# Expert down weights loaded in 32 KB packets, two experts on even and odd partitions

## The reference, cut to what matters

```python
def run_block(args):
    xb, e = args
    h = jax.nn.silu(xb @ w_gate[e]) * (xb @ w_up[e])
    return h @ w_down[e]
```

## Time and profile before

| | us |
|---|---|
| median of 3 runs | 1330.17 |
| lowest and highest | 1329.52, 1331.28 |
| the profiled execution's own time | 1329.42 |
| its span, first to last instruction | 1327.6 |
| busy: TensorE products, VectorE, ScalarE | 966.9, 451.8, 281.9 |

### The profile page before, as it was taken

The page is one execution under the profiler, slowest core; times in us unless marked ns, Lnnn a source line. Parts: engine busy times, 40 slices in busy tenths (PEclk is TensorE's granted clock), DMA queues, the critical chain, the costliest instruction groups (busy, mean ns, idle before and its releaser), DMA issues.

```text
span 1327.6 us, 30597 instructions
## 1 busy us (share of the span) xinstructions
PE 966.9 (73%) x13784; PEld 668.0 (50%) x13784; DVE 451.8 (34%) x1013; ACT 281.9 (21%) x632; POOL 41.8 (3%) x38
## 2 busy tenths in 40 slices
PE   9999999999999876466475746647574664757474
PEld 6998778888866433233243423324342432434242
DVE  4798776788844221111010211101021111102121
ACT  5655343738332100000000010000000000000001
POOL 0000201011120000000000000000000000000000
PEclk9999999999999988788787878878797978879798
DMA  9562455235494999999999999999999999999996
GB/s 329 164 246 82 150 190 190 99 112 203 175 429 177 400 433 431 427 430 433 428 431 438 429 429 435 428 429 431 436 430 434 431 429 428 431 433 432 429 426 270
DMA packets 56023, 464.45 MB, mean 350 GB/s; under 512 B 6250, under 2 KB 15268, under 8 KB 37924
## 3 DMA queue, kind: packets, MB, share of 16 engines
q1 hardware_dynamic: 55040, 460.81, 83.5%
q10 hardware_dynamic: 932, 2.92, 0.6%
HBM read 462.67 MB, written 1.05 MB: 349 GB/s over the span
## 4 chain that ended last, share of the span: by engine, by line
DMA 47%; PE 43%; DVE 6%; ACT 1%; issue 1%; SPq 1%; POOL 0%; POOLq 0%; DVEq 0%; ACTq 0%
DMA second_set<-in_w_up 41%; PE bank L2234 15%; PE bank L2877 9%; DMA ring<-in_w_up 5%; PE bank L2786 5%; PE bank L2769 3%; PE bank L2188 3%; PE bank L2212 2%; DVE ring_lo L1380 1%; PE bank L2282 1%; PE bank L2391 1%; PE bank L2299 1%; PE bank L2416 1%; DVE expert_area L2040 1%; DVE qk L1351 1%
## 5 line engine op out<-in xcount | busy, mean ns | idle before, releaser
L2890 PE MATMUL bank<-consts 128*32 128x32 f32 x52 | 8.0, 247 | 237.9 <-DMA second_set<-in_w_up 170.7
L2234 PE MATMUL bank<-ring_lo,xt_hi 128*128 128x512 f32 (+3 forms) x544 | 171.9, 383 | 0.2 <-DVE ring_lo L1380 0.2
L2786 PE MATMUL bank<-ring,consts 128*32 128x256 f32 x1952 | 118.7, 382 | 69.7 <-DVE consts L2043 41.0
L1266 ACT ACTIVATE expert_area<-bank 128x128 f32<-128x128 f32 x64 | 15.0, 275 | 656.4 <-PE bank L2877 577.6
L2040 DVE TENSOR_TENSOR expert_area<-expert_area,bank 128x128 f32<-128x128 f32 x64 | 22.9, 358 | 340.0 <-ACT expert_area L1266 340.0
L2890 PEld LDWEIGHTS bank<-consts 128*32 128x32 f32 x52 | 4.7, 138 | 245.9 <-DMA second_set<-in_w_up 176.9
L2786 PEld LDWEIGHTS bank<-ring,consts 128*32 128x32 f32 x1952 | 62.7, 109 | 121.8 <-issue 59.9
L2877 PE MATMUL bank<-second_set,expert_area 64*32 64x256 f32 x3328 | 119.4, 452 | 1.1 <-issue 1.1
L2877 PE MATMUL bank<-ring,expert_area 64*32 64x256 f32 x3328 | 118.8, 452 | 0.0
L2234 PEld LDWEIGHTS bank<-ring_lo,xt_hi 128*128 128x128 f32 x544 | 99.1, 188 | 18.4 <-issue 1.5
L2877 PEld LDWEIGHTS bank<-second_set,expert_area 64*32 64x32 f32 x3328 | 70.5, 127 | 44.6 <-issue 26.9
(11 more groups left out here) (351 smaller groups left out, 1400.5 us busy)
## 6 DMA issues: line engine op xcount, KB each, us to landing
ring<-in_w_down SPq DMA_DIRECT2D x60, 2048.0 KB, 22.1
ring<-in_w_gate SPq DMA_DIRECT2D x13, 4096.0 KB, 31.6
ring<-in_w_up SPq DMA_DIRECT2D x13, 4096.0 KB, 40.7
second_set<-in_w_gate SPq DMA_DIRECT2D x13, 4096.0 KB, 32.4
second_set<-in_w_up SPq DMA_DIRECT2D x13, 4096.0 KB, 41.7
ring<-in_w_gate SPq DMA_DIRECT2D x7, 2048.0 KB, 17.7
ring<-in_w_up SPq DMA_DIRECT2D x6, 2048.0 KB, 22.1
ring<-in_moba_w_kv SPq DMA_DIRECT2D x4, 2048.0 KB, 8.4
```

The lines of the kernel that those rows point to most:

```text
L2234: last = nc.tensor.matmul(dst, x[at], w[:, c, :], start=(piece == 0 and c == 0 and w is hi and x is x_hi), stop=(piece == 1 and c == per - ...
L2786: last = nc.tensor.matmul(down_in[SLOTS * j:SLOTS * j + SLOTS, :], turned[:, SLOTS * k:SLOTS * k + SLOTS], w[k][:, 256 * j:256 * j + 256], ...
```

## The change

In the paired rounds the downs of a pair share one buffer, `ring` 4 and 5 together, 32 KB on each partition. The even expert takes the 64 even partitions and the odd expert the 64 odd ones; each is one DMA of 64 rows of 32 KB. A row of the new layout holds 8 of the 512 hidden features. The hidden rows of an expert are written into a 128 x 256 tile at every second column, the other columns being zero, so that after the turn in 32 x 32 blocks the expert's features stand on its own partitions and zeros on the other's. The down product of one expert then runs over all 128 rows of the shared buffer in 8 steps rather than 4. Both downs wait for both down products of the pair before, and TensorE waits for both loads ahead of the first product. Round 15's loads are reordered: gate and up of its first two experts, then their downs. The zero tiles lie in `early_down` and are cleared once on VectorE ahead of the paired rounds.

```diff
-        hidden_pair = [hidden, expert_area[:, 1152:1280]]
+        hidden_zeros = early_down[:, 2048:2560].rearrange("p (w n) -> p w n", w=2)
+        hidden_pair_t = early_down[:, 2560:3072].rearrange("p (w n) -> p w n", w=2)
+        down_pair = ring[:, 4:6, :].rearrange("p k n -> p (k n)")
...
+                frees[2]()
                 for parity in range(2):
-                    frees[2 + parity]()
-                    down(e + parity, ring[:, 4 + parity, :], down_landed[parity])
+                    src = t["w_down_2"][0, bass.ds(e + parity, 1)].rearrange("e (f k) n -> f (e k n)", k=2 * 4)
+                    sp.dma_start(down_pair[parity::2, :], src).then_inc(down_landed[parity], 16)
...
-                        load_pair(e, q, (used, used, down_taken(GROUP * r + (first + 2 * q - 1)),
-                                         down_taken(GROUP * r + (first + 2 * q))))
+                        load_pair(e, q, (used, used, down_taken(e)))
...
-            load_expert(e, 0, hidden_taken(e - 2), down_taken(e - 1))
-            load_expert(e + 1, 1, hidden_taken(e - 2), down_taken(e))
+            hidden_taken(e - 2)()
+            for i in range(2):
+                if i:
+                    hidden_taken(e)()
+                for k, name in enumerate(("w_gate_2", "w_up_2")):
+                    gate_or_up(name, e + i, ring[:, 2 * i + k, :], gate_up_landed[i])
+            down_taken(e)()
+            for i in range(2):
+                down(e + i, ring[:, 4 + i, :], down_landed[i])
...
+                own = hidden_zeros[:, of, :].rearrange("p (k q e) -> p k q e", k=8, e=2)[:, :, :, of]
+                nc.vector.tensor_tensor(own, *gate_up, ALU.mult).then_inc(hidden_ready, 1)
                 dve.wait_ge(hidden_ready, x + 1)
-                nc.vector.transpose(hidden_t_pair[of], hidden_pair[of]).then_inc(hidden_t_ready, 1)
+                nc.vector.transpose(hidden_pair_t[:, of, :], hidden_zeros[:, of, :]).then_inc(hidden_t_ready, 1)
...
+            nc.vector.memset(hidden_zeros, 0.0)
...
+            def down_of_pair(parity):
+
+                for k in range(8):
+                    for j in range(4):
+                        last = nc.tensor.matmul(down_in[SLOTS * j:SLOTS * j + SLOTS, :],
+                                                hidden_pair_t[:, parity, SLOTS * k:SLOTS * k + SLOTS],
+                                                down_pair[:, D * k + 256 * j:D * k + 256 * j + 256],
+                                                start=(k == 0), stop=(k == 7))
+                last.then_inc(down_in_psum, 1)
...
-                        pe.wait_ge(down_landed[parity], 32 * (n - 2) + (16 * q + 16))
+                        if parity == 0:
+                            for landed in down_landed:
+                                pe.wait_ge(landed, 32 * (n - 2) + (16 * q + 16))
                         if i:
                             down_drained(GROUP * n + i)
-                        down(ring[:, 4 + parity, :], range(4), hidden_t_pair[parity])
+                        down_of_pair(parity)
```

More of the change, by code:

```diff
@@ L336, in build @@
         hidden_t = unused[:, 1024:1152]
-        hidden_t_pair = [hidden_t, unused[:, 1408:1536]]
         onehot = unused[:, 1152:1408].rearrange("p (t s) -> p t s", t=2)
@@ L796, in fifth_used @@
                 down_taken(6)()
-            load_pair(8, 0, (hidden_taken(5), fifth_used, hidden_taken(6), down_taken(8)))
-            load_pair(10, 1, (hidden_taken(8), hidden_taken(7), down_taken(9), down_taken(10)))
+            load_pair(8, 0, (hidden_taken(5), fifth_used, down_taken(8)))
+            load_pair(10, 1, (hidden_taken(8), hidden_taken(7), down_taken(10)))
             load_further_pairs(3 * GROUP, ROUNDS - 4)
             e = NE - GROUP
-            load_expert(e, 0, hidden_taken(e - 2), down_taken(e - 1))
-            load_expert(e + 1, 1, hidden_taken(e - 2), down_taken(e))
+            hidden_taken(e - 2)()
[7 more added lines that the diff above has]
+                down(e + i, ring[:, 4 + i, :], down_landed[i])
             load_expert(e + 2, 0, hidden_taken(e + 1), down_taken(e + 1))
@@ L2034, in take_back, with hidden_of_pair, hidden_of @@
                 nc.vector.tensor_copy(back, back_in).then_inc(back_ready, 1)
-            def hidden_of(x, of=0):
+            def hidden_of_pair(x, of):
                 dve.wait_ge(silu_done, x + 1)
-                gate_up = [a.rearrange("p (q k) -> p k q", k=4)
+                gate_up = [a.rearrange("p (q k) -> p k q", k=8)
                            for a in (act_g_pair[of], hidden_pair_in[of][:, P:2 * P])]
-                nc.vector.tensor_tensor(hidden_pair[of].rearrange("p (k q) -> p k q", k=4), *gate_up,
-                                        ALU.mult).then_inc(hidden_ready, 1)
+                own = hidden_zeros[:, of, :].rearrange("p (k q e) -> p k q e", k=8, e=2)[:, :, :, of]
+                nc.vector.tensor_tensor(own, *gate_up, ALU.mult).then_inc(hidden_ready, 1)
                 dve.wait_ge(hidden_ready, x + 1)
-                nc.vector.transpose(hidden_t_pair[of], hidden_pair[of]).then_inc(hidden_t_ready, 1)
+                nc.vector.transpose(hidden_pair_t[:, of, :], hidden_zeros[:, of, :]).then_inc(hidden_t_ready, 1)
+            def hidden_of(x):
+                dve.wait_ge(silu_done, x + 1)
+                gate_up = [a.rearrange("p (q k) -> p k q", k=4) for a in (act_g, hidden_in[:, P:2 * P])]
+                nc.vector.tensor_tensor(hidden.rearrange("p (k q) -> p k q", k=4), *gate_up, ALU.mult).then_inc(
+                    hidden_ready, 1)
+                dve.wait_ge(hidden_ready, x + 1)
+                nc.vector.transpose(hidden_t, hidden).then_inc(hidden_t_ready, 1)
             def drain_down(n, i):
@@ L2078, in paired_round @@
                     for parity in range(2):
-                        hidden_of(GROUP * r + (2 * q + parity), parity)
+                        hidden_of_pair(GROUP * r + (2 * q + parity), parity)
                     for parity in range(2):
@@ L2779, in hidden_turned, with down @@
                 pe.wait_ge(hidden_t_ready, x + 1)
-            def down(down_w, chunks, turned=hidden_t):
+            def down(down_w, chunks):
                 w = down_w if isinstance(down_w, list) else [down_w[:, D * k:D * k + D] for k in range(4)]
@@ L2786, in down @@
                         last = nc.tensor.matmul(down_in[SLOTS * j:SLOTS * j + SLOTS, :],
-                                                turned[:, SLOTS * k:SLOTS * k + SLOTS],
+                                                hidden_t[:, SLOTS * k:SLOTS * k + SLOTS],
                                                 w[k][:, 256 * j:256 * j + 256], start=(k == 0), stop=(k == 3))
```

## The result

The changed kernel takes 1420.66 us (median of 4 runs, 1416.38 to 1421.97) against 1330.15 us of the kernel before measured beside it: a ratio of 1.0672, interval 1.0659 to 1.0685. That is 90.5 us slower, where 1.6 us faster was forecast, and far outside the range. The profiled execution took 1421.64 us, with a span of 1419.8 us.

The account below looks back on a forecast made before the run. The prediction took the paired rounds to be bound by the DMA engines. Larger packets save 1.56 us, all other terms cost nothing, so the median of 1330.17 us becomes 1328.6 us, range 1326.9 to 1334.0 us.

Parts of the forecast that it names:

- What bounds the kernel: Paired rounds of 58.17 us are bound by the DMA engines, DMA share 1.00; other engines wait once per pair.
- the packets: Paired downs: one 32 KB packet replaces two of 16 KB, saving 7.5 ns each, 1.56 us in all (1.1 to 2.4).
- The collision rival: Half-filled 64-row down transfers collide in memory, packets last twice as long: +253 us, 1583 us; chance 0.08.
- More products: Down products grow from 32 to 64 records; a pair is later by 3.5 to 4.5 us, costing nothing on the path.
- the cover: TensorE's idle time before gate and up, 13.1 us at `second_set` and 5.0 us at `ring`, hides the added products.
- Both loads before the first product: TensorE's wait for both downs of a pair adds at most 1 us, out of the same 8 us.
- Later issues: SP issues both downs behind both earlier products, still 8 us early; costs only if TensorE is late by over 8 us.
- The code rival: The paired rounds' longer code is fetched again, 7 packets in 12 rounds: +3.2 to +5.5 us, net +1.6 to +4; chance 0.25.
- No gain: Engine time goes by bytes alone, the 7.5 ns per packet being a recording artefact: 1330.2 us; chance 0.12.
- the small terms: Reordered first and last paired loads and the clearing on VectorE: put at nothing, reaching from 0 to +1 us.

Follow-up runs that it names:

- steps4: The changed kernel with 4 of 8 steps in each paired down product, half the hidden features left out: 1328.05 us, ratio 0.9985 to the kernel before.
- pair_product: The changed kernel with both experts of a pair in one product, 16 products of 512 columns in place of 64 of 256: 1328.19 us, ratio 0.9984.
- double_late_both: The kernel before with paired down products run twice, both downs issued behind both earlier products, and TensorE waiting for both downs: 1403.20 us.
- the last two steps of the table: Adding TensorE's wait for both downs to doubled products with later issue, 1380.43 to 1403.20 us; then from that kernel to the change, 1420.66 us.
- pad20_after: The changed kernel with 20 small products, 80 records, ahead of the loop of paired rounds: 1396.53 us.

## Why the prediction was wrong, point by point

Two steps failed. A code fetch was priced at 0.038 to 0.066 us; TensorE lost 10.0 us per round to nine of them. And each delay was held against the same idle time by itself, so that the downs were taken to be issued 8 us early and the wait for both to cost at most 1 us; with products and code together TensorE stood 7.1 us per round ahead of the downs.

**What bounds the kernel, and the packets: right.** Loads in the new layout save time, 2.3 us in steps4 (0.8 to 3.2 by the interval) and 2.1 in pair_product (0.9 to 3.3), against 1.56 (1.1 to 2.4) forecast; the intervals are too wide to tell 1.56 from 2.2. From the bytes: 224.96 over 224.40 MB is 0.25%, on 13 rounds of 58.17 us 1.9 us. The collision rival falls with the same row.

**More products: the size of one right, the cover wrong.** A down product takes 3.66 us with 64 records (the down at 958.28, and most others), inside 3.5 to 3.86; a round's 43.3 us are over the 41 to 42.5 because the down behind the long wait takes longer, at a lower clock; the turn takes 0.445 us at 256 columns and the strided product 0.358. With fitting code the idle time covers it. The sentence "Were the second cover gone, q = 0 would begin a little late, and the next wait takes that back" had no next wait to go to once the stops had eaten both covers.

**Both loads before the first product: the step that failed next.** "At most 1 us is added to a pair, out of the same 8 us" holds while the downs are issued far ahead. Once they are issued when TensorE already wants them, the second one's landing is exposed: 951.8 against 947.1 us, 4.7 us in a round, and 23 us in all between the two kernels that differ by this wait alone. The rest of the 7.1 us is mostly silu, product and turn, which take 1.5 us where no load is waited for (before the down at 994.27), and 0.8 us for the first down.

**Later issues.** The point named, TensorE late by over 8 us, was the right one, and DMA share under 0.99 the right sign. I asked of each edit by itself whether it reached that point. The edits and the stops share one budget, 18 us of idle time per round (13.1 and 5.0). Products took 8 to 9 us of it and code 10.0, which is all of it; the 7.1 us ahead of the downs came on top and are nearly the 7.5 us by which a round grew.

**The code rival: right in kind, wrong in price, and too low at 0.25.** It is what happened: q8 in every round, with 9 packets where some 7 were counted. The step that failed is "Each costs at least its bytes, 16 KB at 431 GB/s or 0.038 us, and at most its packet time [...] 0.066 us." That prices what the fetch takes from the DMA engines, because they were the bound. The fetch is paid by the engine that waits for the code. TensorE stood still 119.8 us for it, 1.12 us per fetch, 17 times my upper bound. The text even said that the rival "would also show as idle time 'issue'" and gave that idle time no price. The earlier trace rows had one: 0.6% of 16 engines' 66 us over 6 packets is 1.06 us for a packet on the engine that carries it, and 0.066 is the sixteenth part of that. At 1.06 us the 7 packets counted are 7.4 us in a round, and the 9 that came 9.5. Added to the 7 to 9 us by which the prediction made a round's two pairs later, that is 14 to 19 us against 18 of idle time: the rival would have stood at the point where the downs come too late, and not at +1.6 to +4 us.

The Trainium skill, in Runtime: NRT & Kernel Launch, Instruction fetch mechanics, says of a crossing from one block of code to the next that its cost is mostly hidden. In the paired rounds here it isn't hidden, 10 us per round by the waits above, and the measurement decides. The same section warns that a taken branch whose target isn't in the current 2-page window forces a fetch of the target page before execution can go on. The change agrees: it stops at the jump back in every round (3.74 us at 970.43). The kernel before doesn't: its loop of 1583 instructions is far longer than two such pages of 256, and it jumped back 12 times without a fetch.

**No gain and the small terms.** The first and last loads and the clearing cannot be told apart in the changed kernel; in steps4, which has them all, they cost nothing that shows.

What stays open: why double_late_both changes from one sort of round to the other at some 930 us; why three of a round's nine fetches stop TensorE and the others don't; and how much of the 23 and 17 us of the last two steps of the table, which stand as waits ahead of the downs, is the place of the stops, given that a shift of the loop alone moved the time by 24 us.

## What to carry to other kernels

Count the instructions of a loop body before adding to it, and look at q8 in the trace: a loop that shows no fetches may sit 64 instructions under the limit, as here, and past it the whole body is fetched in every pass. Price such a fetch by what the engine that runs the code loses, not by its bytes. When several edits are each hidden by the same idle time, add them up against it once, and ask what is issued late when it is gone; and where a layout doubles the work, look first for a shape that does it in as many instructions or fewer, as one product for both experts did here.

## What was not expected of the hardware

That loop length acts as a step: 1583 instructions stay, 1646 are fetched anew with 9 packets in nearly every round, and 64 ahead of the 1583 are enough to tip a quarter of the rounds. That the length of the stops depends on the load of the DMA engines, 1.12 us per fetch with the loads of the change and 0.37 at an eighth of them. That a stop which falls between the issue of a load and its landing is nearly free, 24 us in pad20_after. And that an odd-looking transfer, 64 rows on every second partition, runs at full rate: 432.6 GB/s over 520 us in steps4, 431.5 in the kernel before.
